# Two token combinations ahead of the block sums and two on GpSimd, in the first pair of three perceptrons

## What is computed

```python
h = h + jnp.square(jax.nn.relu(_rms_norm(h, norm_ff_g[l]) @ ff_w1[l])) @ ff_w2[l]
...
def swiglu(x, w_gate, w_up, w_down):
    return (jax.nn.silu(x @ w_gate) * (x @ w_up)) @ w_down
...
x = layer_norm(ALPHA * x + swiglu(x, ffn_w_gate[layer], ffn_w_up[layer], ffn_w_down[layer]),
               ln_ffn_g[layer], ln_ffn_b[layer])
```

## Time and profile before

| what | value |
|---|---|
| median of 3 runs (lowest to highest) | 1988.3 us (1986.84 to 1988.57) |
| profiled execution: its own time / its span | 1988.44 / 1986.6 us |
| mean granted TensorE clock | 0.991 |
| busy: TensorE, VectorE, ScalarE, GpSimd | 1934.7, 1139.9, 811.7, 377.5 us |

### The profile page before, as it was taken

How to read it: one execution, slowest core, us unless ns; L and a number is a source line. 1 busy time by engine, 2 the same in 40 slices (tenths; PEclk the granted TensorE clock), 3 DMA queues, 4 the chain that set the end, 5 groups by cost and what they waited for, 6 DMA issues and landing times.

```text
span 1986.6 us, 29878 instructions
## 1 busy us (share of the span) xinstructions
PE 1934.7 (97%) x12504; PEld 1282.1 (65%) x12504; DVE 1139.9 (57%) x1547; ACT 811.7 (41%) x1313; POOL 377.5 (19%) x355
## 2 busy tenths in 40 slices
PE   8999999999989999999999999999999998999997
PEld 5655655757666654886577666648765585666576
DVE  6666776655577732245758666523565667656324
ACT  6344311444355521134536344312555544444223
POOL 1011111410143320024014421200500126111101
PEclk9999999999999999999999999999999999999999
DMA  6221200233212322222220323323111022232321
GB/s 248 85 75 55 84 22 22 91 122 107 107 64 85 128 106 97 95 107 86 85 107 22 127 86 128 106 99 135 43 64 53 33 85 101 91 125 88 106 107 43
DMA packets 28241, 179.83 MB, mean 91 GB/s; under 512 B 2961, under 2 KB 7185, under 8 KB 7185
## 3 DMA queue, kind: packets, MB, share of 16 engines
q1 hardware_dynamic: 27312, 170.93, 24.0%
q10 hardware_dynamic: 512, 4.94, 0.7%
q0 software_dynamic: 288, 2.10, 0.3%
HBM read 175.86 MB, written 2.10 MB: 90 GB/s over the span
## 4 chain that ended last, share of the span: by engine, by line
PE 64%; DVE 4%; ACT 1%; issue 0%; DMA 0%; ACTq 0%; DVEq 0%; SPq 0%
PE psum_a L422 16%; PE psum_a L424 16%; PE psum_a L423 16%; PE psum_b L422 4%; PE psum_b L424 4%; PE psum_b L423 4%; PE psum_b L559 2%; DVE ARENA L2018 1%; PE psum_b L1168 1%; PE psum_a L1122 0%; DMA W<-weights 0%; PE psum_a L1187 0%; DVE MIX L2061 0%; PE psum_b L570 0%; PE psum_a L1235 0%
## 5 line engine op out<-in xcount | busy, mean ns | idle before, releaser
L1998 DVE SCALAR_TENSOR_TENSOR W_PARTS<-W,W_PARTS 128x2048 f16<-128x2048 f32 x111 | 254.6, 2296 | 299.0 <-ACT W_PARTS L1343 298.9
L1343 ACT ACTIVATE W_PARTS<-W 128x2048 f16<-128x2048 f32 x111 | 211.0, 1904 | 274.8 <-PE psum_a L424 272.7
L422 PE MATMUL psum_a<-U,W_PARTS 128*128 128x512 f16 (+1 forms) x808 | 304.0, 376 | 1.5 <-DVE U L2115 1.5
L423 PE MATMUL psum_a<-U,W_PARTS 128*128 128x512 f16 (+1 forms) x808 | 303.5, 376 | 0.0
L424 PE MATMUL psum_a<-U,W_PARTS 128*128 128x512 f16 (+1 forms) x808 | 303.4, 376 | 0.0
L422 PE MATMUL psum_a<-ARENA,W_PARTS 128*128 128x256 f16 (+1 forms) x860 | 268.1, 312 | 4.1 <-DVE ARENA L2636 2.3
L424 PE MATMUL psum_a<-ARENA,W_PARTS 128*128 128x256 f16 (+1 forms) x860 | 268.0, 312 | 0.0
L423 PE MATMUL psum_a<-ARENA,W_PARTS 128*128 128x256 f16 (+1 forms) x860 | 268.0, 312 | 0.0
L2942 POOL TENSOR_TENSOR ARENA<-ARENA 128x512 f16<-128x512 f32 x76 | 136.2, 1799 | 398.9 <-ACT ARENA L1477 398.8
L424 PEld LDWEIGHTS psum_a<-U,W_PARTS 128*128 128x128 f16 x808 | 79.5, 98 | 91.9 <-issue 2.7
L422 PEld LDWEIGHTS psum_a<-U,W_PARTS 128*128 128x128 f16 x808 | 79.6, 99 | 89.1 <-issue 6.3
(11 more groups left out here) (376 smaller groups left out, 4069.0 us busy)
## 6 DMA issues: line engine op xcount, KB each, us to landing
W<-weights SPq DMA_DIRECT2D x159, 1024.0 KB, 4.8
CON<-const ACTq DMA_DIRECT2D x1, 3071.5 KB, 10.6
X<-x_in SPq DMA_DIRECT2D x4, 256.0 KB, 3.9
X<-x_in SPq DMA_DIRECT2D x1, 1024.0 KB, 7.9
U<-dft POOLq DMA_DIRECT2D x1, 1024.0 KB, 5.6
ARENA<-dft POOLq DMA_DIRECT2D x1, 1024.0 KB, 5.2
U<-mem_in ACTq DMA_DIRECT2D x1, 1024.0 KB, 4.7
y_out<-U SPq DMA_DIRECT2D x2, 512.0 KB, 2.9
```

Of the source, the lines that this page charges most:

```text
L422: nc.tensor.matmul(out, left(0), right(0), start=first, stop=False, skip_group_check=goes_on)
L423: nc.tensor.matmul(out, left(0), right(1), start=False, stop=False, skip_group_check=goes_on)
L1343: nc.scalar.activation(HOMES[home_of[g]][:, 0, :], W[g % 2][:, :], ACT.Copy, scale=W_SCALE).then_inc(sem("panel_high"), 1)
L1998: nc.vector.scalar_tensor_tensor(out=home[:, 1, :], in0=W[g % 2][:, :], scalar=W_SCALE, in1=home[:, 0, :], op0=ALU.mult, op1=ALU.subtract) ...
```

## The change

The combinations are now numbered V5, V6, V7, V4. VectorE makes V5 and V6 alone and their low parts at once; GpSimd makes V7 and V4 (`v_late`), whose high and low parts follow after the first pair's weights. In the first pair the order on ScalarE and VectorE is another one: there FF's head squares come between the block sums and `sums_low`, `rest_high` comes ahead of the first plain tile, and the head's `hidden_high` comes after the first pair's parts have been read. In later pairs `add_part` 2 comes ahead of `sums_low`. TensorE waits for each combination by itself. In a GLU, GpSimd makes V7, V4 and the low parts of the head's two hidden tiles ahead of `rescale`.

```diff
 (TensorE: first_five, sixth, seventh)
-                    pe.wait_ge(sem("v_low"), 4 * MLPS[M.norm] + 4)
+                    pe.wait_ge(sem("v_low"), 4 * MLPS[M.norm] + 1)
                     one_of_seven("q5")
                     one_of_seven("q2")
                     pe.wait_ge(sem("part_read"), 3 * n + 1)
+                    pe.wait_ge(sem("v_low"), 4 * MLPS[M.norm] + 2)
                     one_of_seven("q6")
...
+                    pe.wait_ge(sem("v_low"), 4 * MLPS[M.norm] + 3)
                     one_of_seven("q7")
...
+                    pe.wait_ge(sem("v_low"), 4 * MLPS[M.norm] + 4)
                     one_of_seven("q4")
 (ScalarE: plain_tile, mlp)
+                if not M.gated:
+                    act.wait_ge(sem("relu_squared"), 2 * (j - 2) + m + 1)
...
-                v_high(M)
-                for j in range(1 if M.gated else 2):
-                    hidden_high(M, j)
+                v_high(M, (V5, V6))
...
+                    else:
+                        rest_high(M, seven)
+                        plain_tile(M, plain, 0)
+                        split(panel_of[(M.name,) + seven] + 1)
+                        plain_tile(M, plain, 1)
+                        for i in range(3):
+                            read_part(M, seven, i)
+                        v_high(M, (V7, V4))
+                        for j in range(1 if M.gated else 2):
+                            hidden_high(M, j)
 (VectorE: v_made, mlp)
-                v5, v6, v4, v7 = (M.v32[:, v] for v in range(4))
...
+                    last = nc.vector.tensor_tensor(out, src[:, even, first], src[:, even, second], ALU.subtract)
...
+                    last = nc.vector.tensor_tensor(out, M.v32[:, V5], src[:, odd, second], ALU.add)
...
-                v_low(M)
-                block_sums(M, M.pairs[0][1])
+                v_low(M, (V5, V6))
...
                         finish(M, before, 0)
-                    sums_low(M, seven)
-                    if before:
                         add_part(M, before, 2)
+                        sums_low(M, seven)
                         finish(M, before, 1)
...
+                    else:
+                        raw_low(M, seven)
+                        block_sums(M, seven)
+                        if not M.gated:
+                            for j in range(2):
+                                for half in range(2):
+                                    hidden(j, half)
+                        sums_low(M, seven)
+                        rest_low(M, seven)
+                        split(panel_of[(M.name,) + seven] + 1)
+                        v_low(M, (V7, V4))
                     if not M.gated:
                         hidden(plain[1])
                     add_part(M, seven, 0)
 (GpSimd: new v_late, layer_norm)
+            def v_late(M, src):
+                even, odd, first, second = slice(0, KT, 2), slice(1, KT, 2), *HALVES
+                pool.wait_ge(sem(f"high_{M.norm}"), 16)
+                pool.wait_ge(sem(f"gained_{M.norm}"), 16)
+                v7, right = M.v32[:, V7], src[:, odd, second]
+                if M.norm in BIAS:
+                    for i in range(4):
+                        last = nc.gpsimd.tensor_scalar(v7[:, i, :], src[:, 2 * i, second], par(BIAS[M.norm], 2 * i), None, ALU.add)
+                    link(last)
+                    nc.gpsimd.tensor_tensor(v7, v7, right, ALU.subtract).then_inc(sem("v_late"), 1)
+                else:
+                    nc.gpsimd.tensor_tensor(v7, src[:, even, second], right, ALU.subtract).then_inc(sem("v_late"), 1)
+                pool.wait_ge(sem("v_made"), 2 * MLPS[M.norm] + 2)
+                nc.gpsimd.tensor_tensor(M.v32[:, V4], M.v32[:, V6], src[:, odd, first], ALU.subtract).then_inc(sem("v_late"), 1)
...
                     odd_low(name)
+                    if name in MLPS:
+                        v_late((GLU0, GLU1)[NORMS_LN.index(name) // 2], X)
+                        mlp((GLU0, GLU1)[NORMS_LN.index(name) // 2], 0, 2)
                     rescale(name)
```

More of the change, by code:

```diff
@@ L51 @@
 A11, A12, S1, S2, S4, A22, S3 = range(7)
-V5, V6, V4, V7 = range(4)
+V5, V6, V7, V4 = range(4)
 PRODUCTS = ("q1", "q5", "q2", "q6", "q3", "q7", "q4")
@@ L1947, in _ @@
             gr_copy(2)
-            act.wait_ge(sem("mla_kr_ready"), 4)
+            act.wait_ge(sem("mla_kr_ready"), 5)
             for tt in range(4):
@@ L2031, in rest_low, with v_made @@
                 block_low(M, A22, S3 + 1, W[g % 2][:, 2 * BLOCK:4 * BLOCK], "panel_high", g + 1, "panel_low")
-            def v_made(M, src):
-                at = 4 * MLPS[M.norm]
+            def v_made(M, src, v):
+                at = 2 * MLPS[M.norm]
                 even, odd, first, second = slice(0, KT, 2), slice(1, KT, 2), *HALVES
-                v5, v6, v4, v7 = (M.v32[:, v] for v in range(4))
[L2038 to L2050, removed]
-                else:
-                    last = nc.vector.tensor_tensor(v7, src[:, even, second], src[:, odd, second], ALU.subtract)
@@ L2053, in v_made, with v_low @@
+                out = M.v32[:, v]
+                if v == V5:
+                    dve.wait_ge(sem(f"high_{M.norm}"), 16)
+                    dve.wait_ge(sem(f"gained_{M.norm}"), 16)
+                    last = nc.vector.tensor_tensor(out, src[:, even, first], src[:, even, second], ALU.subtract)
+                else:
+                    dve.wait_ge(sem("v_made"), at + V5 + 1)
+                    last = nc.vector.tensor_tensor(out, M.v32[:, V5], src[:, odd, second], ALU.add)
                 last.then_inc(sem("v_made"), 1)
[L2055 to L2061, removed]
+            def v_low(M, vs):
+                at = 4 * MLPS[M.norm] + 1
+                for v in vs:
+                    dve.wait_ge(sem("v_high"), at + v)
+                    nc.vector.scalar_tensor_tensor(out=V16[:, 1, v], in0=M.v32[:, v], scalar=-1.0 if v in (V6, V7) else 1.0, in1=V16[:, 0, v],
@@ L2292, in mlp @@
                 split(head_panel(M.norm, 2))
-                v_made(M, X if M.gated else NT)
+                src = X if M.gated else NT
+                v_made(M, src, V5)
+                v_made(M, src, V6)
                 if M.gated:
                     hidden(0, 1)
[L2296 to L2299, removed]
-                v_low(M)
-                block_sums(M, M.pairs[0][1])
+                v_low(M, (V5, V6))
                 before = None
@@ L2935, in _, with mlp @@
                     nc.gpsimd.tensor_tensor(HY[:, ct, :], HY[:, ct, :], HY[:, 4 + 4 * o + ct, :], ALU.mult).then_inc(sem("z_gated"), 1)
-            def mlp(M):
-                pool.wait_ge(sem("v_made"), 4 * MLPS[M.norm] + 4)
-                for n in range(2 * M.groups):
+            def v_late(M, src):
[8 more added lines that the diff above has]
+                    nc.gpsimd.tensor_tensor(v7, v7, right, ALU.subtract).then_inc(sem("v_late"), 1)
+                else:
+                    nc.gpsimd.tensor_tensor(v7, src[:, even, second], right, ALU.subtract).then_inc(sem("v_late"), 1)
+                pool.wait_ge(sem("v_made"), 2 * MLPS[M.norm] + 2)
+                nc.gpsimd.tensor_tensor(M.v32[:, V4], M.v32[:, V6], src[:, odd, first], ALU.subtract).then_inc(sem("v_late"), 1)
+            def mlp(M, first=0, end=None):
+                if not M.gated:
+                    pool.wait_ge(sem("v_late"), 2 * MLPS[M.norm] + 2)
+                for n in range(first, end or 2 * M.groups):
                     pool.wait_ge(sem("hidden_high"), tiles_before[M.name] + n + 1)
@@ L3002, in _ @@
             layer_norm("ln_mix0")
-            mlp(GLU0)
+            mlp(GLU0, 2)
             layer_norm("ln_ffn0")
@@ L3018, in _ @@
             layer_norm("ln_mix1")
-            mlp(GLU1)
+            mlp(GLU1, 2)
             layer_norm("ln_ffn1")
```

41 lines of the change are left out of this document (21 added, 20 removed).

## The result

The changed kernel took 1990.62 us (median of 20 runs, 1986.35 to 1992.14), the kernel before, beside it, 1986.96 (20 runs): ratio 1.0017, 95% interval 1.0010 to 1.0024. It is slower by a little, 3.4 us by the ratio (2.0 to 4.8 by its interval). The forecast was 2.5 us faster.

What follows compares the result with a forecast made beforehand. TensorE was taken as the bound, busy 1934.7 of 1986.6 us. FF's +1.3 and 1.9 saved in each of two GLUs gave -2.5 against 1988.44, so 1985.9, as a median 1985.8; range 1976 to 1992.

Steps and rivals of the forecast that it cites:

- The view and the place: TensorE's waits by releaser in the first pairs, 18.6 us, and the low clock behind them; q4's start to compare.
- Collisions: On VectorE beside GpSimd: a wide GpSimd instruction costs VectorE between nothing and 0.6 x 2.95 = 1.8 us.
- I take the middle, 1090.1: GLU's q5 start, taken between 1089.1 and 1091.1, with 7.8 us of GpSimd work charged at 0.6, up to 4.7.
- Rival 3: A wide GpSimd instruction keeps VectorE out for its whole 2.95 us: sum +10.6, about 1999 us; chance 0.12.
- The clock in the GLUs: At each GLU's q4, a 2.7 us wait was taken to drop the clock, at unchanged cost.
- q4 in the GLUs: After q6's end at 1094.1, a 10.7 us chain puts q4 at 1104.8, 1.9 us earlier in each GLU.
- FF: First perceptron: q4 at 600.2, 1.0 us earlier after a 6.7 us wait, plus 2.3 of low clock: +1.3 us.
- What was costed at nothing: `rescale` behind the hidden tiles, weights loaded sooner, later pairs' `add_part` 2 ahead of `sums_low`, the merged semaphore: 0 us.
- its bounds for FF and the GLUs: FF from -4.3, then +1.7, to +2.6, then +2.6; one GLU's q4 from -4.0 to +0.2 us.
- FF's upper bound, 603.7: FF's q4 start with all GpSimd collisions counted: +2.6, then +2.6 us for the low clock.
- its chain to q4: From q6's end through part reads, sums, raw low part and `finish` to the last addition: 14.7 us in FF, 10.7 per GLU.

Runs made afterwards that it cites:

- the earlier trace: Changed kernel with ScalarE's high parts of FF's four head tiles moved between the second and third part read: 1988.66 us, ratio 1.0014.
- the late combinations alone: Changed kernel with `add_part` 2 put back behind `sums_low` in all pairs: 1997.65 us, ratio 1.0052 to the kernel before.
- the additions first: Changed kernel with the first pair's `add_part` 1 and 2 directly behind `add_part` 0, ahead of the second pair's sums: 1973.99 us, ratio 0.9936.
- the narrow one: Changed kernel with the first pair's additions moved ahead, and each GpSimd subtraction split into four of 128 x 256: 1969.09 us, ratio 0.9908.

## Why the prediction was wrong

- **The view and the place were right.** The time lies in TensorE's waits at q5 and q4 and the low clock behind them; q1's waits went, FF's q5 waits 1.77 (1.7 forecast), its q4 is the long one with the half-clock work behind it, `hidden(2)` waits for GpSimd.
- **The step that failed is "Collisions", and from it "I take the middle, 1090.1".** I charged 0.6 of all GpSimd time, 7.8 us, as a ceiling of 4.7; the middle, 1090.1, holds 3.7 of it on top of 1086.4. The runs show another rule: the additions (0.92 each alone, not 0.48) cost next to nothing, a wide subtraction (2.35 us alone, not 2.95) costs 2.16, nearly whole. The 0.6 came from a row in which VectorE's instruction had begun 0.5 us into GpSimd's (582.41 against 581.90) and lost only its rest. The result was 4.3, in a low part and the raw low part, near the ceiling by chance. q5 waits 2.00 us in each GLU and not 1.0 (1090.1 - 1089.1); of this 1.0, the collisions are 0.6, and in GLU0 0.4 is that VectorE began V5 0.7 later than forecast and TensorE q1 only 0.3 later (1074.97 for 1074.26, 1088.00 for 1087.7). Rival 3's rule was the right one for the subtractions; its time was not, because it charged the additions too: 4.3 of 7.8, below its 6.9. The rule of the Trainium skill, "SBUF — State Buffer", section "SBUF: two separate sides", is that of a VectorE instruction with two SBUF inputs and a GpSimd instruction the first to start holds the shared ports for its whole length. The wide subtractions agree (2.16 of 2.35); the additions, which are held up while VectorE runs on, do not show it, nor does a subtraction in FF before the change that was held up through four instructions of VectorE (last section).
- **The clock in the GLUs.** I judged it by q4 alone, between a wait of 3.88 that dropped it and "one of 1.5" that "did not". Behind the 2.0 at q5 it fell, in GLU0 and in GLU1: 1.7 each, not in the sum. GLU0's q4 then kept its clock, GLU1's did not. GLU1 came out at +1.3 instead of -1.9, GLU0 at -1.3. That GLU0 is so near is luck: its waits are 1.7 longer than forecast (5.4 for 3.7), and its low clock cost 1.7 at q5 instead of 2.6 at q4.
- **q4 in the GLUs** was nearly right in its length: from the third part's read (1097.27) to the addition's end (1108.40) 11.1 us, forecast 10.7. It began 3.2 us late (forecast 1094.1), 1.4 with q5 and 1.7 for the half clock behind q5. These also put back TensorE, so q4 waits 3.43 for a forecast 2.7.
- **FF** was mis-sized by 1.8. `hidden(2)` is two squares, not one, and took 3.13 where the sum has 0.64, since GpSimd's low parts run beside it (1.28 in the earlier trace rows). But the first began behind one low part and not behind two, so from q6's end to the first addition the chain is 0.8 longer than forecast (7.9 for 7.1). The wait at q4 was 7.94 instead of 6.7, the low clock cost 2.9 instead of 2.3: +3.1 instead of +1.3.
- **What was costed at nothing** (`rescale`, the loads, the later pairs) cost nothing that shows: the ledger leaves no rest beyond the interval.
- **The range.** Added up as they stand, its bounds for FF and the GLUs (-10.6 and +5.6) give 1978 to 1994 and not 1980 to 1992; FF's upper bound, 603.7, is not worked out there. The result lies inside either.
- **What the prediction did not see** is that its chain to q4 was not necessary. It counted four sums, a raw low part and `finish` ahead of the last addition as given. The addition's place was worth 9.7 us in the kernel before, and the late combinations used that up.

## What to carry to other kernels

List, for each wait of the bounding engine, what stands between the released instruction and its input on the engine that releases it; work for a later consumer in between is the first thing to move, and costs one line. GpSimd is no free engine beside VectorE: count a collision per VectorE instruction, at up to one whole GpSimd subtraction each, so keep its instructions narrow, or put its work where VectorE idles and no product waits for what it makes. Price a wait together with the low clock behind it, and test the parts of a change apart: here a loss of 10.3 us and a gain (9.7 in the kernel before, 7 beside the late combinations) hid behind +3.4.

## What was not expected of the hardware

- GpSimd's additions of a per-partition value (one tensor input) leave VectorE alone, which ran at 1.21 and 1.30 us beside them, but are themselves held up: 6.79 us for four that take 0.92 each alone. GpSimd's wide subtractions of two tensors held VectorE for 2.16 us each in the GLUs.
- The kernel before had shown both sides of this. A `rescale` instruction (one tensor input) took 5.96 us beside four low parts on VectorE, which lost nothing. In FF a subtraction of two tensors was held up too, 5.83 us for 1.15 to 1.6 elsewhere, while the four low parts beside it took their 4.62. So a subtraction does not always get its turn, and a count of one per VectorE instruction is an upper bound. What decides it was not tried.

```profile
1080.13 5.96 POOL L2969 TENSOR_SCALAR X<-X 128x256 f32<-128x256 f32 x1
```

```profile
1080.17 4.62 DVE L2061 SCALAR_TENSOR_TENSOR MIX<-ARENA,MIX 128x1024 f16<-128x1024 f32 x4
```

```profile
572.99 5.83 POOL L2942 TENSOR_TENSOR ARENA<-ARENA 128x512 f16<-128x512 f32 x1 [11.12 <-ACT ARENA L1477]
```

- A wait of 2.0 us at a GLU's q5 was followed by a stretch at 1.2 GHz in each of the eight cases in the profiles (the changed kernel, the late combinations alone, the head tiles earlier, the additions first); FF's waits of 1.8 to 1.9 at q5 were not in any of five (those four kernels and the narrow one). What differs ahead of the two was not tried.
- The same wait of 3.43 us at q4 was followed by the low clock in GLU1 and not in GLU0 of the changed kernel, and in both GLUs with V7 and V4 on VectorE and with FF's head tiles earlier.
